# First weights in quarters, norm gains inside the constants, and five edits in the last block

## The chip, the cores and the metric

The kernel is one program on one core of a Trainium2 chip. A core has a matmul engine (TensorE, PE), a vector engine (VectorE, DVE), an activation engine (ScalarE, ACT), a general engine (GpSimd, POOL) and a queue engine that here only issues DMAs (SyncE, SP). They run beside one another and meet through semaphores. The metric is the device time of one execution in microseconds; lower is better. A run is given as the median of its executions.

## The reference, cut to what matters

256 tokens of width 1024 go through two layers and a last block. All is float32.

```python
for l in range(2):
    proj = rms_norm(x, attn_norm[l]) @ w_in[l]             # 1024 -> 2472
    ...                                                    # mLSTM, latent attention, spatial gating
    x = x + y @ w_out[l]
    x = x + hier_moe(rms_norm(x, ffn_norm[l]), ...)        # 32 experts, two for each token
# the last block
proj = rms_norm_2(x, norm_w) @ w_in_2                      # 1024 -> 6144
qa, ka, va, za, qb, kb, vb, zb, gl_a, gl_b = split(proj)   # 8 times 512, twice 1024
qa, ka = rms_norm_2(heads(qa), q_norm_w), rms_norm_2(heads(ka), k_norm_w)
oa = softmax_attention(qa, ka, va, rel_bias)               # 8 heads, bias by distance, from a table of 32 buckets
ob = stick_breaking_attention(qb, kb, vb)
ya, yb = (oa * silu(za)) @ w_up_moba, (ob * silu(zb)) @ w_up_sb
y = sigmoid(gl_a + b0) * ya + sigmoid(gl_b + b1) * yb
x = x + y @ w_out
```

## The kernel before, in words

The program keeps x on chip, as two tiles of 128 tokens (t = 0, 1). Each engine runs one long list of instructions in program order. Weights come from memory in units of up to 2 MB (a "unit" is 1024 rows by up to 512 columns) into a ring of six slots; SP issues their DMAs in a fixed order and waits before each for the slot to be given back by PE (`freed`), while PE waits for `landed`. Matmul results go to eight banks; an order written out by hand (`MIXER_BANKS`, `second_banks`) says who uses which bank when, PE waits for the bank's last reader (`open_bank`), and `copied(engine, plan, names)` makes an engine wait until the named results have been read out of their banks. A float32 product of 128x128 by 128xN is two passes of PE.

**The start.** SP's first DMAs are, in order: the first 129 columns of the constants (identity and one column of -0.5), x tile 0, the layers' norm gains (L579), the last block's gains (L580), rows 0 to 511 of unit 2 of the first projection (L583), x tile 1, rows 512 to 1023 of unit 2, then unit 3 (L649) and sixteen small loads of the mixer (L608). Constants and gains share the semaphore `loaded_first`; PE, ACT, DVE and POOL wait for 48 of it, three DMAs. PE fills the time with nine products of zeros (`keep_warm`), turns x tile 0 (L1008), ACT scales the result by the gains into `xfT` (L1706), and PE begins `b1t0`, the first result of unit 2, with its first four of eight row blocks k when `loaded_half` is there. It then turns x tile 1, does the other four blocks after `landed[2]`, and goes on with tile 1. Before the mixer's small products (L1129) it waits for all sixteen small loads; POOL waits for the same loads at L778.

**The last block: bias.** After the projections qa, ka, qb and kb, PE turns the bias table (result `rel`), DVE copies it out, PE multiplies it by a bucket matrix to get a row of 384 biases for each of 8 heads (result `f`, L1565), and DVE copies that out (L2617) and raises `f_ready`. Only then does PE multiply va and vb, two tiles each (L1523). SP, which stands at `expand_bias` between the loads of zb and ga0, waits for `f_ready` and writes the rows, each 128 times, into a scratch tensor in memory (`skew`, L701, 1536 KB), waits for that write, and reads it back with a pitch one element short, so that each partition gets its own shift (`s_bias`, L705, 1024 KB). The next four unit loads (ga0, ga1, gb0, gb1, L683) stand behind it on SP. On DVE the normalisation of q and k (L2623, L2627) follows the copy of `f`; then DVE waits for `s_bias` (`bias_moved`) and for the merge gate's bias before the first head.

**The last block: heads.** PE turns q and k (L1574), waits until ACT has copied out all of vb1, qT0, qT1, kT0, kT1 among others, and runs the steps h = 0 to 8. Step h is: `lead` chunks, `first_stage(h)` (logits of both attentions), `front` chunks, `second_stage(h - 1)` (sums of the log rows, which wait for `s_log_ready`, and the turned softmax, which waits for `s_norm_ready`), further chunks, and at every second step `third_stage` (products with v). Chunks are pieces of independent work: one eighth of a tile of za, zb, ga or gb, and `step_tiles` says how many stand where. A lead has one chunk. DVE adds the bias to head h's logits (L2666), gets the maximum, ACT takes the exponential (L1981), DVE scales the rows by the sum (L2656, L2657).

**The end.** The products with w_up (L1657) are gated on DVE to y, turned by PE (`turn_y`, L1645), copied out by ACT, and multiplied with w_out in four results out0 to out3 of 128x512 (L1672). y tile 1 is turned after out1. DVE adds each result to x (L2739). SP stores x tile 0 (512 KB) after out1 and x tile 1 (512 KB) after out3 (L724).

Of the kernel before, what the change touches and what calls it, by code (L numbers as in the profile page):

```python
# [21 lines left out]
P = 128  # L22
SEQ = 256
NT = SEQ // P
D = 1024
# [12 lines left out]
FIRST_CONSTS = P + 1  # L38
# [27 lines left out]
CONST_WIDTHS = [("ident", P), ("neg_half", 1), ("upto", P), ("before", P), ("fromon", P), ("ones", P), ("iota", P),  # L66
# [19 lines left out]
def step_tiles(h):  # L86

    def pieces(first, last):
        out = []
        while first < last:  # L90
            stop = min(last, (first // KD + 1) * KD)
            out.append((TILES[first // KD], first % KD, stop - first // KD * KD))
            first = stop
        return out

    front = h * KD + max(h - 1, 0) * BACK_CHUNKS
    back = front + KD - (TAIL_CHUNKS if h == S_HEADS else 0)
# [10 lines left out]
def second_banks():  # L108
    uses = [("rs", 6), ("rel", 4), ("f", 5)]
    uses += [(n, b) for names in (("qa0", "qa1", "ka0", "ka1"), ("qbA", "qbB", "kbA", "kbB"),  # L110
                                  ("va0", "va1", "vb0", "vb1")) for b, n in enumerate(names)]
    uses += [("qT0", 4), ("qT1", 5), ("kT0", 6), ("kT1", 7)]
    tile = 0

    def opened(pieces):
        nonlocal tile
        for name, k0, _ in pieces:
            if k0 == 0:
                uses.append((name, tile % 4))
                tile += 1  # L120

    for h in range(S_HEADS + 1):
        if h < S_HEADS:
            uses += [(f"z{h}", 4 + h % 2), (f"sc{h}", 6 + h % 2)]
        lead, front, behind, tail = step_tiles(h)
        opened(lead + front)
        if h:
            uses += [(f"r{h - 1}", 4 + (h - 1) % 2), (f"pT{h - 1}", 6 + (h - 1) % 2)]
        opened(behind)
        if h and h % 2 == 0:  # L130
            uses += [(f"ob{h // 2 - 1}", 5), (f"oa{h // 2 - 1}", 7)]
        opened(tail)
    uses += [(f"y{a}{t}{n}", 2 * (n % 2) + (a == "b")) for t in range(2) for n in range(2) for a in "ab"]
    uses += [(f"yT{u}", 4 + u) for u in range(4)] + [(f"out{b}", b) for b in range(4)]
    return uses


def constant_table():
# [18 lines left out]
        "row_limit": np.where(p == 0, SEQ - 1.0, NO_TOKEN),  # L157
        "piece": np.concatenate([(p + P * c) // M_DIM == h for h, c in PIECES], axis=1),
# [41 lines left out]
def program(nc, io, out, mixer=True, second=True):  # L200
    with ExitStack() as ctx:
# [11 lines left out]
        at = 0  # L213
        for name, w in CONST_WIDTHS:
            const[name] = consts[:, at:at + w]
            at += w
# [19 lines left out]
        gain_cols = sb("gain_cols", [P, DEPTH + 1, KD])  # L236
# [179 lines left out]
        loaded_half = sem("loaded_half")  # L416
# [31 lines left out]
        loaded_merge_bias = sem("loaded_merge_bias")  # L448
# [139 lines left out]

# [140 lines left out]
        def _(pool):  # L729
# [33 lines left out]
            for l in range(DEPTH):  # L763
                m = PER * l
                if mixer:
                    if l == 0:
                        pool.wait_ge(loaded_first, 48)
# [102 lines left out]
        def _(pe):  # L870
# [124 lines left out]
            pe.wait_ge(loaded_first, 48)  # L995
# [26 lines left out]
            def mix(l):  # L1022
# [16 lines left out]
                def token_unit(u, name, t, k0=0, k1=KD, release=None):  # L1039
# [5 lines left out]
                    if l == 0 and name == "b1t0" and k0 == 0:  # L1045
                        pe.wait_ge(loaded_half, 16)
                    elif k0 == 0 or name == "b1t0":
                        lands(u, 1)
# [64 lines left out]
                token_unit(2, "b1t0", 0, 0, 4)  # L1113
# [355 lines left out]
            def last_block():  # L1469
# [107 lines left out]
                copied(pe, plan, "qbA", "qbB", "kbA", "kbB", "va0", "va1", "vb0", "vb1", "qT0", "qT1", "kT0", "kT1")  # L1577
# [104 lines left out]
        def _(act):  # L1682
# [14 lines left out]
            def norm_turn(m):  # L1697

                if m == 0:
                    act.wait_ge(loaded_first, 48)  # L1700
                    act.activation(stats[:, 15:16], ident[:, 0:1], ACT.Copy)
# [304 lines left out]
        def _(dve):  # L2006
# [505 lines left out]
            dve.wait_ge(loaded_first, 48)  # L2512
# [70 lines left out]
            def last_block():  # L2583
# [64 lines left out]
                dve.wait_ge(loaded_merge_bias, 16)  # L2648
# [85 lines left out]
                for t in range(NT):  # L2734
                    for n in range(2):
                        name = f"out{2 * t + n}"
                        src = full(dve, plan, name)
                        xs = x[:, t, n * HALF:(n + 1) * HALF]
                        dve.tensor_tensor(xs, xs, src[:, :], ALU.add).then_inc(left(plan, name), 1)  # L2739
                        copied(dve, plan, name)  # L2740
                        if (t, n) == (0, 1):
# [32 lines left out]
```

## Time and profile before

| | |
|---|---|
| median of 3 runs | 1051.71 us (1049.93 to 1052.14) |
| profiled execution | 1053.72 us |
| its span, first to last instruction | 1051.5 us |
| PE busy / DVE / ACT / POOL | 98% / 38% / 27% / 9% |
| chain that ended last | PE 88%, SP's queue 7%, DMA 2%, ACT 1%, DVE 1% |
| mean granted PE clock | 0.998 |
| read from memory | 286.99 MB, 277 GB/s over the span |

Busy shares are of the span. The chain that ended last is followed back from the last instruction, at each step to what released it. A granted clock of 1.00 is 2.4 GHz, of 0.50 1.2 GHz. In a timeline each row gives the start and the length in microseconds, the engine, the line, the operation, what it writes and reads, how many instructions are merged, and in brackets how long the engine had been idle before and what ended that.

### The profile page before, as it was taken

What the parts mean: (1) busy time and instruction counts of PE and PEld (TensorE: products, weight loads), DVE (VectorE), ACT (ScalarE), POOL (GpSimd) and SP (SyncE); (2) the same over time, 40 slices, a digit from 0 to 9 for tenths busy, and PEclk for the clock granted to TensorE, in tenths of its full rate; (3) what the DMA queues carried; (4) which work ended last, traced back from release to release, by engine and by line L of the source; (5) the groups of instructions that cost most, each with busy time, mean ns of one, the idle gap of its engine ahead of it and who ended that gap; (6) DMA issues with size and microseconds to landing.
All of it is one profiled execution on the core that took longest, in us unless ns stands there. A gap on an engine that the chain in (4) does not pass through costs nothing.

```text
span 1051.5 us, 12900 instructions
## 1 busy us (share of the span) xinstructions
PE 1031.5 (98%) x4599; PEld 535.9 (51%) x4599; DVE 397.2 (38%) x970; ACT 279.3 (27%) x540; POOL 97.9 (9%) x144
## 2 busy tenths in 40 slices
PE   8999999999999999999999999999999999999998
PEld 4787654333333434777654333333334756855443
DVE  2362343443344441452343444344431221445221
ACT  4355331111111113354341111111112004565200
POOL 1320221000000002210220000000000200000000
PEclk9999999999999999999999999999999999999999
DMA  8646258999999997245258999999979626842000
GB/s 294 223 147 253 80 200 307 411 411 413 412 411 411 414 368 241 74 176 225 81 201 324 412 411 413 413 411 412 414 300 368 253 29 148 324 161 80 0 1 40
DMA packets 95325, 280.44 MB, mean 267 GB/s; under 512 B 15957, under 2 KB 29699, under 8 KB 86960
## 3 DMA queue, kind: packets, MB, share of 16 engines
q1 hardware_dynamic: 90208, 273.27, 68.5%
q0 software_dynamic: 5072, 6.56, 1.8%
q8 instruction: 29, 0.48, 0.2%
q14 instruction: 16, 0.13, 0.0%
HBM read 286.99 MB, written 4.72 MB: 277 GB/s over the span
## 4 chain that ended last, share of the span: by engine, by line
PE 88%; SPq 7%; DMA 2%; ACT 1%; issue 1%; DVE 1%; DVEq 0%; ACTq 0%
PE bank L935 17%; PE bank L1523 11%; PE bank L964 9%; PE bank L1051 9%; PE bank L886 6%; SPq L598 5%; PE bank L1254 5%; PE bank L1066 4%; PE bank L875 3%; PE bank L1501 3%; PE bank L1672 3%; PE bank L1541 3%; PE bank L1657 3%; DMA ring<-in_w 2%; SPq L604 1%
## 5 line engine op out<-in xcount | busy, mean ns | idle before, releaser
L935 PE MATMUL bank<-ring,arena 128*64 128x512 f32 x1024 | 228.5, 596 | 1.5 <-DMA ring<-in_w 1.5
L935 PEld LDWEIGHTS bank<-ring,arena 128*64 128x64 f32 x1024 | 71.1, 137 | 132.8 <-issue 124.1
L964 PE MATMUL bank<-ring,arena 128*64 128x512 f32 x512 | 116.9, 598 | 0.0
L1523 PE MATMUL bank<-ring,xfT 128*128 128x512 f32 x256 | 113.4, 596 | 0.0
L1051 PE MATMUL bank<-ring,xfT 128*128 128x384 f32 (+2 forms) x256 | 96.1, 526 | 2.5 <-DMA ring<-in_w_in 2.5
L886 PE MATMUL bank<-arena 128*128 128x512 bf16 x384 | 93.3, 379 | 0.0
L1694 ACT ACTIVATE arena<-bank 128x512 bf16<-128x512 f32 (+1 forms) x64 | 38.2, 597 | 190.4 <-PE bank L964 190.4
L2025 DVE TENSOR_TENSOR arena<-bank,arena 128x512 f32<-128x512 f32 x60 | 41.5, 691 | 119.4 <-ACT arena L1694 119.4
L1523 PEld LDWEIGHTS bank<-ring,xfT 128*128 128x128 f32 x256 | 47.4, 190 | 55.5 <-issue 55.0
L964 PEld LDWEIGHTS bank<-ring,arena 128*64 128x64 f32 x512 | 33.9, 136 | 68.4 <-issue 68.4
L1051 PEld LDWEIGHTS bank<-ring,xfT 128*128 128x128 f32 x256 | 47.7, 192 | 40.0 <-issue 26.6
L1687 ACT ACTIVATE arena<-bank,arena 128x256 f32<-128x256 f32 x32 | 15.2, 475 | 198.6 <-PE bank L935 198.5
L839 POOL DMA_INDIRECT arena<-x_store,arena x30 | 30.7, 1024 | 370.8 <-PE bank L875 355.3
L2046 DVE SCALAR_TENSOR_TENSOR arena<-arena,bank 128x256 f32<-128x256 f32 x32 | 15.4, 480 | 113.2 <-ACT arena L1687 113.2
L1254 PE MATMUL bank<-ring,xfT 128*128 128x512 f32 x128 | 57.4, 596 | 0.0
L875 PEld LDWEIGHTS bank<-consts,arena 128*128 128x128 f32 x240 | 31.3, 195 | 48.7 <-issue 48.7
L886 PEld LDWEIGHTS bank<-arena 128*128 128x128 bf16 x384 | 37.8, 99 | 32.5 <-issue 1.6
L1066 PE MATMUL bank<-xfT,ring 128*128 128x256 f32 x192 | 43.0, 380 | 0.0
L875 PE MATMUL bank<-consts,arena 128*128 128x128 f32 x240 | 42.7, 300 | 0.0
L2037 DVE TENSOR_TENSOR arena<-bank,row_gain 128x512 f32<-128x512 f32 x60 | 41.2, 687 | 3.5
L1066 PEld LDWEIGHTS bank<-xfT,ring 128*128 128x128 f32 x192 | 36.2, 190 | 5.3
L2031 DVE TENSOR_TENSOR arena<-arena 128x512 bf16<-128x512 f32 x60 | 38.5, 682 | 0.0
(383 smaller groups left out, 1161.6 us busy)
## 6 DMA issues: line engine op xcount, KB each, us to landing
ring<-in_w SPq DMA_DIRECT2D x256, 512.0 KB
ring<-in_w SPq DMA_DIRECT2D x64, 1024.0 KB, 12.7
ring<-in_w_in SPq DMA_DIRECT2D x14, 2048.0 KB, 19.8
ring<-in_w_in SPq DMA_DIRECT2D x8, 1536.0 KB, 13.9
ring<-in_w_out SPq DMA_DIRECT2D x6, 2048.0 KB
x_store<-x POOLq DMA_DIRECT2D x4, 512.0 KB, 6.1
ring<-in_w_up_moba SPq DMA_DIRECT2D x1, 2048.0 KB
ring<-in_w_up_sb SPq DMA_DIRECT2D x1, 2048.0 KB
```

The costliest lines, as they stand in the source:

```text
L598: sp.dma_start(up_view(s)[:, i, w].rearrange("p k f -> p (k f)"), src)\
L875: ins = pe.transpose(dst[:, i * P:(i + 1) * P], x_rows[:, buf, :].rearrange("p (i k) -> p k i", k=KD)[:, k, :], ident)
L886: ins = pe.matmul(bank[2 * t + n][:, :], onehotT[:, par, t * P:(t + 1) * P], y_parts[:, par, i, n, :], start=False, stop=False, skip_group ...
L935: ins = pe.matmul(bank[5][CELL * e:CELL * (e + 1), :], xg[:, par, 4 * h + k, at:at + CELL], view[:, e, :, k, :], start=(h == 0 and k == 0) ...
L964: ins = pe.matmul(bank[5 + n][CELL * e:CELL * (e + 1), :], turned[:, par, c, CELL * e:CELL * (e + 1)], down_view(s)[:, e, c, n * HALF:(n + ...
L1051: ins = pe.matmul(dst[:, 0:w], xfT[:, k, t * P:(t + 1) * P], unit_view(u, w)[:, k, :], start=(k == 0), stop=(k == KD - 1))
L1066: ins = pe.matmul(dst[:, at:at + SEQ], unit_view(u, M_WIDTH)[:, k, c * P:(c + 1) * P], xfT[:, k, :], start=(k == 0), stop=(k == KD - 1))
L1254: ins = pe.matmul(bank[plan[name][0]][:, :], xfT[:, k, t * P:(t + 1) * P], unit_view(n, HALF)[:, k, :], start=(first and k == ks[0]), stop ...
L1523: ins = pe.matmul(dst[:, :], xfT[:, k, t * P:(t + 1) * P], w[:, k, :], start=(k == 0), stop=(k == KD - 1))
L2025: dve.tensor_tensor(y_rest[:, n, :], bank[5 + n][:, :], y_parts[:, par, 0, n, :], ALU.subtract)\
L2031: dve.tensor_tensor(y_parts[:, par, 2, n, :], y_rest[:, n, :], y_parts[:, par, 1, n, :], ALU.subtract).then_inc(S["low_ready"], 1)
L2037: dve.tensor_tensor(xg[:, par, 4 * half:4 * half + 4, :], src[:, :].rearrange("p (k s) -> p k s", k=4), row_gain_in[:, 4 * half:4 * half + ...
```

## The change

Seven edits:

1. The three rows of norm gains (24 columns) are laid into the constants on the host, behind the column of -0.5; the first DMA brings 153 columns instead of 129, and the two gain DMAs are gone. All waits for `loaded_first` are for 16 instead of 48.
2. Unit 2's first half is loaded in two quarters (blocks k 0, 1 and 2, 3), x tile 1 after them, then the second half. `b1t0` waits for each quarter.
3. The second quarter's semaphore also serves the merge gate's bias, whose waiter on DVE now wants 32.
4. `rel` is turned after va's tile 0, `f` is multiplied after the first four blocks of va's tile 1.
5. The first step's lead has two chunks instead of one, and the wait for vb1, qT0, qT1, kT0 and kT1 stands behind it.
6. `turn_y(1)` stands between out0 and out1.
7. The last result is cut in two of 256 columns (out3, out4), and x tile 1 is stored in three parts: columns 0 to 511, 512 to 767, 768 to 1023, each after its own result.

```diff
-FIRST_CONSTS = P + 1
+FIRST_CONSTS = P + 1 + 3 * 8
...
-    lead = front + (1 if h < S_HEADS else 0)
+    lead = front + (2 if h == 0 else 1 if h < S_HEADS else 0)
...
+OUTPUTS = [[("out0", 0, 0, HALF), ("out1", 1, 0, HALF)],
+           [("out2", 0, 0, HALF), ("out3", 1, 0, HALF // 2), ("out4", 1, HALF // 2, HALF)]]
...
-        loaded_merge_bias = sem("loaded_merge_bias")
+        loaded_second_quarter = sem("loaded_second_quarter_and_merge_bias")
+        loaded_merge_bias = loaded_second_quarter
...
             sp.dma_start(x[:, 0, :], io["x"][0, 0:P, :]).then_inc(loaded_x[0], 16)
-            sp.dma_start(gain_cols[:, 0:DEPTH, :], io["attn_norm"]).then_inc(loaded_first, 16)
-            sp.dma_start(gain_cols[:, DEPTH, :], io["norm_w_2"]).then_inc(loaded_first, 16)
-            for half in range(2):
-                c0, c1 = UNIT_COLS[2]
-                sp.dma_start(unit_view(2, c1 - c0)[:, 4 * half:4 * half + 4, :],
-                             io["w_in"][0, half * HALF:(half + 1) * HALF, c0:c1].rearrange("(k p) n -> p k n", p=P))\
-                  .then_inc(loaded_half if half == 0 else landed[2], 16)
-                if half == 0:
+            c0, c1 = UNIT_COLS[2]
+            for k0, k1, signal in ((0, 2, loaded_quarter), (2, 4, loaded_second_quarter), (4, 8, landed[2])):
+                if k0 == 4:
                     sp.dma_start(x[:, 1, :], io["x"][0, P:2 * P, :]).then_inc(loaded_x[1], 16)
+                sp.dma_start(unit_view(2, c1 - c0)[:, k0:k1, :],
+                             io["w_in"][0, k0 * P:k1 * P, c0:c1].rearrange("(k p) n -> p k n", p=P)).then_inc(signal, 16)
...
-            for t in range(NT):
-
-                sp.wait_ge(x_tile_ready if t == 0 else x_ready, last)
-                sp.dma_start(out[0, t * P:(t + 1) * P, :], x[:, t, :]).then_inc(stored, 16)
-            sp.wait_ge(stored, 16 * NT)
+            parts = [(0, 0, D, x_tile_ready, last)]
+            if second:
+                parts += [(1, 0, HALF, x_tile_ready, last + 1), (1, HALF, HALF + HALF // 2, x_tile_ready, last + 2),
+                          (1, HALF + HALF // 2, D, x_ready, last)]
+            else:
+                parts += [(1, 0, D, x_ready, last)]
+            for t, c0, c1, signal, n in parts:
+                sp.wait_ge(signal, n)
+                sp.dma_start(out[0, t * P:(t + 1) * P, c0:c1], x[:, t, c0:c1]).then_inc(stored, 16)
+            sp.wait_ge(stored, 16 * len(parts))
...
-                token_unit(2, "b1t0", 0, 0, 4)
+                token_unit(2, "b1t0", 0, 0, 2)
+                token_unit(2, "b1t0", 0, 2, 4)
...
-                pe.wait_ge(loaded_second, 4 * 16)
-                pe.wait_ge(rel_ready, 1)
-                dst = open_bank("rel")
-                done(pe.transpose(dst[0:33, 0:S_HEADS], s_rel[0:S_HEADS, :], ident[0:S_HEADS, 0:S_HEADS]), "rel")
-                copied(pe, plan, "rel")
-                dst = open_bank("f")
-                done(pe.matmul(dst[0:S_HEADS, 0:384], s_relT[0:33, :], buckets[0:33, :], start=True, stop=True), "f")
-                for u in ("va", "vb"):
-                    for t in range(NT):
-                        token_tile(u, t)
...                                                # the same instructions in bias_rows() and bias_table()
+                token_tile("va", 0)
+                bias_rows()
+                token_tile("va", 1, k1=4)
+                bias_table()
+                token_tile("va", 1, k0=4)
+                for t in range(NT):
+                    token_tile("vb", t)
...
-                copied(pe, plan, "qbA", "qbB", "kbA", "kbB", "va0", "va1", "vb0", "vb1", "qT0", "qT1", "kT0", "kT1")
+                copied(pe, plan, "qbA", "qbB", "kbA", "kbB", "va0", "va1", "vb0")
...
                     chunks(lead)
+                    if h == 0:
+                        copied(pe, plan, "vb1", "qT0", "qT1", "kT0", "kT1")
...
                 for t in range(NT):
-                    if t:
-                        turn_y(t)
                     copied(pe, plan, f"yT{2 * t}", f"yT{2 * t + 1}")
-                    for n in range(2):
-                        dst = open_bank(f"out{2 * t + n}")
+                    for name, n, c0, c1 in OUTPUTS[t]:
+                        if name == "out1":
+                            turn_y(1)
+                        dst = open_bank(name)
                         for k in range(KD):
-                            ins = pe.matmul(dst[:, :], xfT[:, k, t * P:(t + 1) * P], outs[n][:, k, :],
+                            ins = pe.matmul(dst[:, 0:c1 - c0], xfT[:, k, t * P:(t + 1) * P], outs[n][:, k, c0:c1],
                                             start=(k == 0), stop=(k == KD - 1))
-                        done(ins, f"out{2 * t + n}")
+                        done(ins, name)
...
-                dve.wait_ge(loaded_merge_bias, 16)
+                dve.wait_ge(loaded_merge_bias, 32)
```

## Rows read from the trace of the kernel before

**Rows 1.** The page, busy time by engine: us, share, instructions.
```profile
PE 1031.5 (98%) x4599; PEld 535.9 (51%) x4599; DVE 397.2 (38%) x970; ACT 279.3 (27%) x540; POOL 97.9 (9%) x144
```
**Rows 2.** The chain that ended last, in order of time: start, length, what.
```profile
2.58 6.51 DMA ring<-in_w_in
...
13.17 8.54 PE bank L1051 x24
```
**Rows 3.** Timeline of SP's queue at the start.
```profile
1.63 0.42 SPq L579 DMA_DIRECT2D gain_cols<-in_attn_norm  x1
...
2.58 0.43 SPq L583 DMA_DIRECT2D ring<-in_w_in  x1
...
3.60 0.44 SPq L583 DMA_DIRECT2D ring<-in_w_in  x1
```
**Rows 4.** Windows: stretch, PE, PEld, DVE, ACT, POOL busy, PEclk, DMA share, GB/s.
```profile
4.00:4.50 0.50, 0.50 (x3) 0.20 (x2) 0.00 (x0) 0.00 (x0) 0.00 (x0) 1.00 0.84 96
```
**Rows 5.** The chain in the last block, up to head 0's second stage.
```profile
849.61 0.85 issue
...
850.88 0.81 PE bank L1565 x2
851.69 27.68 PE bank L1523 x64
...
879.39 2.65 ACT arena L1948 x5
...
898.54 0.43 PE bank L1600 x2
```
**Rows 6.** Timeline of SP's queue and DVE in the last block.
```profile
852.36 0.31 SPq L701 DMA_DIRECT2D skew<-arena  x1
...
884.27 0.36 SPq L705 DMA_DIRECT2D arena<-skew  x1
...
889.60 0.29 DVE L2666 SCALAR_TENSOR_TENSOR spare<-bank,arena 128x128 f32<-128x128 f32 x1 [31.79 <-DMA arena<-skew]
...
893.61 0.35 DVE L2657 TENSOR_SCALAR spare<-spare,arena 128x256 f32<-128x256 f32 x1
```
**Rows 7.** Timeline of PE, DVE and SP's queue at the end.
```profile
986.45 0.42 DVE L2709 TENSOR_TENSOR arena<-bank,arena 128x256 f32<-128x256 f32 x1 [2.96 <-PE bank L1620]
...
1033.56 13.97 PE L1672 MATMUL bank<-ring,xfT 128*128 128x512 f32 x32 [0.78 <-ACT xfT L1948]
...
1047.64 0.69 DVE L2739 TENSOR_TENSOR x<-x,bank 128x512 f32<-128x512 f32 x1 [6.25 <-PE bank L1672]
1048.42 0.36 SPq L724 DMA_DIRECT2D out<-x  x1
```
**Rows 8.** DMA issues at the end: count, KB each, median us to landing.
```profile
out<-x SPq DMA_DIRECT2D x2, 512.0 KB, 2.6
```
**Rows 9.** Timeline of ACT, PE and POOL at the start.
```profile
5.64 2.18 ACT L1706 ACTIVATE xfT<-bank,gain_cols 128x128 f32<-128x128 f32 x8 [0.51 <-PE bank L1008]
...
9.22 3.08 PE L1051 MATMUL bank<-ring,xfT 128*128 128x424 f32 x8 [2.53 <-DMA ring<-in_w_in]
...
10.68 0.78 POOL L742 DMA_DIRECT2D consts<-in_consts  x1 [10.25 <-DMA x<-in_x]
...
27.77 1.72 POOL L778 TENSOR_TENSOR arena<-cos_sin,arena 128x32 f32<-128x32 f32 x8 [13.64 <-DMA arena<-in_a_w_ukv]
...
28.96 0.53 PE L1129 MATMUL bank<-consts,arena 5*128 5x5 f32 x6
```
**Rows 10.** Windows in the middle of the skew write.
```profile
865.00:870.00 5.00, 5.00 (x13) 2.28 (x12) 0.00 (x0) 0.69 (x1) 0.00 (x0) 1.00 0.44 51
```
**Rows 11.** Timeline of PE where layer 1 begins.
```profile
399.10 2.64 PE L1008 MATMUL bank<-consts,x 128*128 128x128 f32 x16 [2.60 <-issue]
```
**Rows 12.** Windows of PE alone: stretch, busy, PEclk, DMA share, GB/s.
```profile
400.00:425.00 25.00, 25.00 (x81) 0.93 0.91 305
```
**Rows 13.** Windows during the last store.
```profile
1050.00:1050.50 0.50, 0.00 (x0) 0.00 (x0) 0.00 (x0) 0.00 (x0) 0.00 (x0) 1.00 1.00 410
```

More of the change, by code:

```diff
@@ L64 @@
 HALF = 512
-CONST_WIDTHS = [("ident", P), ("neg_half", 1), ("upto", P), ("before", P), ("fromon", P), ("ones", P), ("iota", P),
+CONST_WIDTHS = [("ident", P), ("neg_half", 1), ("gains", 3 * 8), ("upto", P), ("before", P), ("fromon", P), ("ones", P), ("iota", P),
                 ("causal", 2 * P), ("inv_freq", 16), ("rev", NE), ("cell64", NE),
@@ L133, in second_banks @@
     uses += [(f"y{a}{t}{n}", 2 * (n % 2) + (a == "b")) for t in range(2) for n in range(2) for a in "ab"]
-    uses += [(f"yT{u}", 4 + u) for u in range(4)] + [(f"out{b}", b) for b in range(4)]
+    uses += [(f"yT{u}", 4 + u) for u in range(4)] + [(f"out{b}", b) for b in range(5)]
     return uses
@@ L157, in constant_table @@
         "row_limit": np.where(p == 0, SEQ - 1.0, NO_TOKEN),
+        "gains": full * np.zeros((1, 3 * 8)),
         "piece": np.concatenate([(p + P * c) // M_DIM == h for h, c in PIECES], axis=1),
@@ L213, in program @@
         at = 0
+        gain_cols = consts[:, P + 1:FIRST_CONSTS].rearrange("p (m k) -> p m k", m=DEPTH + 1)
         for name, w in CONST_WIDTHS:
@@ L235, in program @@
         spare = sb("spare", [P, D])
-        gain_cols = sb("gain_cols", [P, DEPTH + 1, KD])
         rstd_row = spare[:, 6 * P:6 * P + SEQ]
@@ L415, in program @@
         loaded_first = sem("loaded_first")
-        loaded_half = sem("loaded_half")
+        loaded_quarter = sem("loaded_quarter")
         loaded_positions = sem("loaded_positions")
@@ L766, in _ @@
                     if l == 0:
-                        pool.wait_ge(loaded_first, 48)
+                        pool.wait_ge(loaded_first, 16)
                     norm(l)
@@ L994, in _ @@
             keep_warm(9)
-            pe.wait_ge(loaded_first, 48)
+            pe.wait_ge(loaded_first, 16)
             def turn(m, tiles=range(NT)):
@@ L1045, in token_unit @@
                     if l == 0 and name == "b1t0" and k0 == 0:
-                        pe.wait_ge(loaded_half, 16)
-                    elif k0 == 0 or name == "b1t0":
+                        pe.wait_ge(loaded_quarter, 16)
+                    elif l == 0 and name == "b1t0" and k0 == 2:
+                        pe.wait_ge(loaded_second_quarter, 16)
+                    elif k0 in (0, 4):
                         lands(u, 1)
@@ L1557, in last_block, with bias_rows, bias_table @@
                 pair_unit("kb")
-                pe.wait_ge(loaded_second, 4 * 16)
-                pe.wait_ge(rel_ready, 1)
-                dst = open_bank("rel")
-                done(pe.transpose(dst[0:33, 0:S_HEADS], s_rel[0:S_HEADS, :], ident[0:S_HEADS, 0:S_HEADS]), "rel")
-                copied(pe, plan, "rel")
-                dst = open_bank("f")
-                done(pe.matmul(dst[0:S_HEADS, 0:384], s_relT[0:33, :], buckets[0:33, :], start=True, stop=True), "f")
-                for u in ("va", "vb"):
-                    for t in range(NT):
-                        token_tile(u, t)
+                def bias_rows():
+                    pe.wait_ge(loaded_second, 4 * 16)
+                    pe.wait_ge(rel_ready, 1)
+                    dst = open_bank("rel")
+                    done(pe.transpose(dst[0:33, 0:S_HEADS], s_rel[0:S_HEADS, :], ident[0:S_HEADS, 0:S_HEADS]), "rel")
+                def bias_table():
+                    copied(pe, plan, "rel")
+                    dst = open_bank("f")
+                    done(pe.matmul(dst[0:S_HEADS, 0:384], s_relT[0:33, :], buckets[0:33, :], start=True, stop=True), "f")
+                token_tile("va", 0)
[5 more added lines that the diff above has]
+                    token_tile("vb", t)
                 pe.wait_ge(s_qk_ready, 1)
@@ L1699, in norm_turn @@
                 if m == 0:
-                    act.wait_ge(loaded_first, 48)
+                    act.wait_ge(loaded_first, 16)
                     act.activation(stats[:, 15:16], ident[:, 0:1], ACT.Copy)
@@ L2511, in _ @@
             dve.nop().then_inc(main["low_ready"], 2)
-            dve.wait_ge(loaded_first, 48)
+            dve.wait_ge(loaded_first, 16)
             for t in range(NT):
@@ L2734, in last_block @@
                 for t in range(NT):
-                    for n in range(2):
-                        name = f"out{2 * t + n}"
+                    for name, n, c0, c1 in OUTPUTS[t]:
                         src = full(dve, plan, name)
-                        xs = x[:, t, n * HALF:(n + 1) * HALF]
-                        dve.tensor_tensor(xs, xs, src[:, :], ALU.add).then_inc(left(plan, name), 1)
+                        xs = x[:, t, n * HALF + c0:n * HALF + c1]
+                        dve.tensor_tensor(xs, xs, src[:, 0:c1 - c0], ALU.add).then_inc(left(plan, name), 1)
                         copied(dve, plan, name)
-                        if (t, n) == (0, 1):
+                        if name in ("out1", "out2", "out3"):
                             dve.nop().then_inc(x_tile_ready, 1)
@@ L2764 @@
     arrays["consts"], arrays["late_consts"] = constant_table()
-    arrays["attn_norm"] = np.ascontiguousarray(arrays["attn_norm"].reshape(DEPTH, KD, P).transpose(2, 0, 1))
-    arrays["norm_w_2"] = np.ascontiguousarray(arrays["norm_w_2"].reshape(KD, P).transpose(1, 0))
+    gains = np.concatenate([arrays.pop("attn_norm").reshape(-1, P), arrays.pop("norm_w_2").reshape(-1, P)])
+    arrays["consts"][:, P + 1:FIRST_CONSTS] = gains.transpose(1, 0)
     io = {name: nc.dram_tensor(f"in_{name}", a.shape, mybir.dt.from_np(a.dtype), kind="ExternalInput").ap()
```

## The prediction

> **What bounds the kernel now.** I read the page first: TensorE (PE) is busy for 98% of the span [rows 1], so almost any stall of PE is paid in full and work beside PE is free until it makes PE wait. The change touches three places, and I read each as a chain of waits or a timeline.
>
> *The start.* PE's first real matmuls begin at 9.22, released by the first half of the unit, issued at 2.58 and 6.51 us under way [rows 2]. Ahead of it on SP's queue stand four DMAs; each takes a slot of about 0.47 us [rows 3]. Two of them are the gains, 12 KB in all, and the stream has a hole at 4.0 to 4.5, 96 GB/s, between x tile 0 and the weights [rows 4].
>
> *The last block.* From 849.61 to 851.69 PE works almost nothing: transpose, DVE's copy, table product [rows 5]. At 879.39 it stands behind five ACT copies, 2.65 us. A second path runs beside: the table (`f`) goes to DVE, DVE frees SP, SP issues the skew write at 852.36, and only at 884.27 the read back. DVE, idle for 31.79 us, starts head 0 at 889.60, when the read has landed [rows 6].
>
> *The end.* PE waits 0.78 us for ACT's copies before tile 1's output products; then come an add of 0.69 us, the issue at 1048.42, and 2.6 us to the landing of 512 KB [rows 7, 8].
>
> Times are of the profiled execution: 1051.5 us of span, 2.2 us around it, 1053.72 in all, 2.0 above the median 1051.71 of the three runs. I take differences and add them to the median.
>
> **The start, worked.** The first quarter is issued at 1.63, 0.95 us earlier than the half was; the second at 2.10, x tile 1 at 2.58, the last half at about 3.1 instead of 3.60 [rows 3]. The hole closes, so weights land between 0.5 (issue alone) and 0.95 us (stream shifted whole) earlier, and a quarter needs half of the bytes. PE also needs the turned x: ACT's eight copies start at 5.64 and take 2.18, the first four are out at 6.7 [rows 9]. So PE starts at about 6.9. Eight passes at 0.36 (24 in 8.54 [rows 2]) last to 9.8, the turn of tile 1 to 10.7; x tile 1, in at about 10.3 before (POOL, waiting for it, issues at 10.68 [rows 9]), is there. Next comes the last half. Before, PE found it there at 13.17. Its 0.87 MB at some 390 GB/s behind x tile 1 put its landing at 12.5; 0.5 to 0.95 earlier is 11.55 to 12.0. PE waits there, a new wait of about a microsecond, and the gain is 13.17 - 11.7 = **-1.5**. Bounds: -0.5 (it landed just at 13.17 and moves by its issue alone) and -2.4 (no wait: 13.17 - 10.75). The next place is the mixer's small loads: POOL gets them at 27.77, PE needs them at 28.96 [rows 9]; PE comes at 27.5, they at 27.3 or before, so nothing is lost. Later units wait for PE's frees, so the shift passes through. The 96 bytes more per partition in the constants and the waits for 16 instead of 48 cost nothing: PE, ACT and DVE all waited for x or for each other anyway. The merge bias wait for 32 instead of 16 counts a quarter that landed 800 us before.
>
> **The bias products.** Of the 2.08 us from 849.61 to 851.69, PE keeps the table product (two passes, 0.64 of array time at 0.43 x 384/512 each) and a small transpose (0.15); the stalls go: **-1.3**. But `f` is now made after va's tile 0 and half of tile 1: 27.68/4 + 27.68/8 + 0.2 = 10.6 us after 849.61, at 860.2 instead of 850.88 [rows 5]: 9.3 us later. Behind it on DVE wait only the q/k normalisations: they ended 31.79 before 889.60, at 857.8, now 867.1, and PE wants them at 878: free. Behind it on SP wait the skew write, the read, and the loads of ga0 to gb1, which PE needs only two heads, some 20 us, later. The write takes 31.6 us with the DMAs otherwise empty (51 GB/s, share 0.44 [rows 10]), so no neighbour slows it and nothing shortens it when it is later. DVE's start moves to 898.9, its normalised head 0, ready at 893.61 + 0.35 [rows 6], to 903.25.
>
> A rule of the Trainium skill speaks otherwise. "DMA: Bandwidth & Descriptors", section "Why a DMA increments its semaphore by 16 and not by 1", has a DMA spread over the largest number of engines, up to 16, that divides its slowest dimension: 8 here. That agrees with the share of 0.44. By the same page of the Trainium skill, section "Specifications", an engine moves about 27 GiB/s, which would make the 1.57 MB take an estimated 6.8 us, and then the delay would be hidden and the sum that of the second rival below. The row's 51 GB/s decides.
>
> **Copies' wait and the lead of two chunks.** PE's transposes now end at 879.8, the second lead chunk (0.87 each: four passes of 256 columns, half of 27.68/64 apiece [rows 5]) at 881.5, after ACT's last copy at 880.8. Head 0's products start 1.9 us earlier than before, and one chunk less stands between them and the second stage: PE would reach it at 895.8, 2.75 before 898.54; 1.3 of that are the bias stalls, **-1.45** the copies. There PE meets DVE. It stalls, first for DVE's log rows (until about 901.9), does their small products, waits for the normalised head until 903.25, and after three transposes (0.33) resumes its chunks at 903.6; before it resumed at 899.6 (the row at 898.54 and 1.2 us of stage). So the block turns from -2.75 into **+4.05**, with a PE gap of 6 us. About 0.4 more follows at head 2: its banks come free only after head 1's turn on ACT and DVE, about 4.3 us like head 0's (889.60 to 893.96), so near 907.5, where PE comes at 907.2. Bounds of the block: -2.75 (data in time) and +5.5 (write and read 1 us longer).
>
> **The clock.** After the gap of 2.60 us before 399.10 the granted clock of the stretch 400 to 425 is 0.93, so part of it went at 1.2 instead of 2.4 GHz: 25 x 0.07 = 1.75 us lost [rows 11, 12]. The gap of 2.53 us before 9.22 brought no fall: the passes after it take 0.36 for 424 columns [rows 2, 9]. No gap of 6 us is in this trace; by the nearest row I take 1.5, with bounds of 0 and 3.5 (twice that row). It overlaps the 0.4 of head 2, so block and clock are **+5.6**. The Trainium skill, "TensorE: Matmul & The Clock Gate", Part 1, says that idleness sends the array back to 1.2 GHz and work brings it up again; by that rule the fall is nearly certain, and the first rival out.
>
> **The end.** Turning y tile 1 between out0 and out1 hides ACT's copies under out1: -0.8 [rows 7]; its rows are ready on DVE long before. The last add is of 256 columns: 0.42 for 0.69, -0.27 [rows 7]. The last store is 128 KB: 384 KB less at 410 GB/s is -0.95 [rows 8, 13]; between -0.5 (a floor of 2.1 us to landing) and -0.95 I take -0.85. Two products of 256 columns instead of one of 512 are the same array time. Earlier stores are issued 3.4 us before and are out of the way. Together **-1.9**, bounds -1.2 and -2.1.
>
> **Sum.** -1.5 + 5.6 - 1.9 = +2.2: 1051.7 + 2.2 = **1053.9**.
>
> **Rivals.**
> *The clock stays up.* For it: the unpunished gap at 9.22. Against: twice as long a gap here. +4.45 in the block: +1.1, 1052.8.
> *The bias data come in time: faster.* One mechanism: the skew write takes less time when it starts later, or its landing is not what DVE waited for. It decides from a write and read shorter by 7.4 us (PE would come at 895.8, DVE's result at 903.25). Then -1.5 - 2.75 - 1.9 = -6.15: 1045.6. For it: half-used DMA engines. Against: an even 51 GB/s in an empty stretch and an idle of 31.79 that ends with that landing.
> *The start gives little.* The last half lands as before but for its issue (-0.5), and the small loads hold PE at 27.3: +3.2, 1054.9. For it: both transfers move with bytes, not with PE. Against: the hole in the stream.
>
> **How the numbers follow.** 0.2% is 2.1 us, about what this measurement can tell from none. Forecast 0.52, alone from 1052.3 to 1056; clock stays up 0.25; bias data in time 0.10; poor start 0.08; rest 0.05. The range must take in most of the first two and their unknown terms: 1050.7 to 1056.2. Above 1053.8 lie rather more than half of the forecast, the poor start and a little of the second case, 0.44; within 0.2% the rest of these, 0.44; faster 0.12.
>
> **What would show it.** PE's first weights matmul near 6.9 and a new DMA wait before the k = 4 product near 11.7. No stall around 850 and at the ACT copies. `f`'s copy 9 us later against va0, the skew write still 31.6 us, DVE idle before head 0 for about 31.8 us, and a PE stall of 6 us before the second stage of head 0, followed by a granted clock of 0.50. At the end no wait before out2, a landing under 2 us. I am wrong if the write is shorter, if no stall stands at the second stage, or if the start moves by more than 2.4 us.

## The result and the profile after

The changed kernel takes 1055.99 us (median of 5 runs, 1055.24 to 1060.11) against 1051.53 (5 runs) for the kernel before: ratio 1.0053, 95% interval 1.0040 to 1.0065. Run again later in the same form it gave 1.0048 (1.0034 to 1.0062). So it is slower by about 5 us, with 3.6 to 6.8 as what the two intervals allow. Forecast were +2.2 and a range up to 1056.2: the direction holds, the size is more than double.

The profiled execution is the slowest of the first five, 1060.11 us; its span is 1057.8. The second profile, of the repetition, took 1058.90 (span 1056.6), and stands beside the first wherever the clock matters. PE is busy 98% of the span as before [rows 1]:

```profile
PE 1036.3 (98%) x4615; PEld 541.2 (51%) x4615; DVE 397.3 (38%) x971; ACT 279.1 (26%) x540; POOL 97.9 (9%) x144
```

*Start.* PE's timeline of the changed kernel (start, length, engine, line, operation, out<-in, count, idle before and what ended it):

```profile
7.16 3.11 PE L1061 MATMUL bank<-ring,xfT 128*128 128x424 f32 x8
10.11 1.04 PE L1016 MATMUL bank<-consts,x 128*128 128x128 f32 x8
11.50 2.73 PE L1061 MATMUL bank<-ring,xfT 128*128 128x424 f32 x7 [0.36 <-DMA ring<-in_w_in]
...
27.53 0.53 PE L1140 MATMUL bank<-consts,arena 5*128 5x5 f32 x6
```

The first weights matmul starts 2.06 us earlier than the one at 9.22 [rows 9]. A new wait for a DMA stands before k = 4, the second half of the unit, and what followed at 13.17 [rows 2] follows at 11.50. The small transposes stand at 27.53 instead of 28.96 [rows 9]. These are differences of one profile from one; several profiles of either start make them smaller, as worked out below.

*The last block.* The chain of the changed kernel between va and head 0's second stage (start, length, what):

```profile
849.33 6.87 PE bank L1534 x16
856.19 0.12 PE bank L1574
856.32 3.63 PE bank L1534 x8
859.95 0.75 PE bank L1579 x2
...
861.35 33.63 DMA skew<-arena
894.98 0.02 issue
895.00 5.92 DMA arena<-skew
...
903.63 0.30 DVE arena L2704
...
904.07 1.19 PE bank L1619 x2
...
906.76 4.98 PE bank L1512 x16
```

The stalls of [rows 5] around the bias products are gone. The chain now runs over DMAs: `f` at 859.95, the skew write at 861.35 instead of 852.36, the read at 895.00 instead of 884.27 [rows 6], head 0's log rows (L2704) ready at 903.94. What PE waited for in this stretch (engine and line, releaser: total, times, longest):

```profile
PE bank L1619 <- DVE arena L2704: 8.4, 1, 8.4
```

PE came at 904.07 - 8.4 = 895.7, where the forecast had 895.8. DVE was later than forecast. The windows show the clock (stretch, PE busy, PEclk, DMA share, GB/s):

```profile
900.00:904.00 4.00, 0.00 (x0) 0.50 1.05 388
904.00:910.00 6.00, 5.93 (x18) 0.52 1.05 387
```

The granted clock is already at the 1.2 GHz level while PE stands, and the work behind the wait runs at it: the stage's first two products take 1.19 us, and 16 chunk products 4.98.

*The end*, timeline of the changed kernel, and its DMA issues (KB each, us to landing):

```profile
1034.29 20.81 PE L1693 MATMUL bank<-ring,xfT 128*128 128x512 f32 x64
...
1055.13 0.42 DVE L2759 TENSOR_TENSOR x<-x,bank 128x256 f32<-128x256 f32 x1 [3.03 <-PE bank L1693]
```
```profile
out<-x SPq DMA_DIRECT2D x2, 128.0 KB, 1.8
```

PE no longer waits before tile 1's products, which was 0.78 us [rows 7], the last add is 0.42 instead of 0.69, and the last store lands in 1.8 us instead of 2.6 [rows 8].

**One yardstick for all traces.** I cut each profiled execution at two places that every kernel here has: where the last block's norm begins on PE (16 turns of x, at 791.85 before), and where the first 12 products with the unit ga0 begin behind head 2's turn (918.35 before). Between them lies "the block", behind the second "the end". In us, as differences from the kernel before (126.50 and 133.15):

```
kernel                        block    end     skew write
changed, first profile        +8.83   -2.24   33.6
changed, second profile       +7.82   -2.2    33.6
bias products late, alone     +6.20   -0.1    31.9
bias products back            -1.52   -2.2    33.6
start edits alone              0.00   -0.1    34.45
copies' wait and lead alone   -1.52    0.0    31.9
end edits alone                0.00   -2.2    31.9
```

The block and the end repeat to 0.1 us where nothing is late, so the profiles split what the times, which scatter by 3 us, can't.

### The profile page after: what moved, and what is told of

Its sections match the earlier page's. It is cut to its first block, busy times and chain, and to the rows that moved or that the text cites. A ratio compares the mean times of both kernels' runs of the same rounds, so it can differ in the third digit from the quotient of the medians.

```text
span 1057.8 us, 12934 instructions
## 1 busy us (share of the span) xinstructions
PE 1036.3 (98%) x4615; PEld 541.2 (51%) x4615; DVE 397.3 (38%) x971; ACT 279.1 (26%) x540; POOL 97.9 (9%) x144
## 4 chain that ended last, share of the span: by engine, by line
PE 77%; SPq 12%; DMA 8%; issue 2%; ACT 1%; DVE 0%; DVEq 0%; ACTq 0%
PE bank L943 14%; SPq L601 9%; PE bank L1534 9%; PE bank L1061 8%; PE bank L972 7%; PE bank L894 5%; PE bank L1265 5%; PE bank L1076 4%; DMA ring<-in_w 3%; DMA skew<-arena 3%; SPq L607 3%; PE bank L1552 3%; PE bank L1693 3%; PE bank L1678 3%; PE bank L883 2%
```

## The experiments

Ratios are to runs of the kernel before, taken beside each experiment on the same chip; 0.001 is 1.05 us. Code is cut at "...".

**Bias products back** in front of va, all else changed.

```diff
-token_tile("va", 0)
 bias_rows()
-token_tile("va", 1, k1=4)
 bias_table()
-token_tile("va", 1, k0=4)
-for t in range(NT):
-    token_tile("vb", t)
+for u in ("va", "vb"):
+    for t in range(NT):
+        token_tile(u, t)
```

> The changed kernel with the bias products back ahead of va, all other edits kept. Theory (the late table costs the time): the skew write starts near 851 again, head 0 on DVE near 889, no PE wait at the second stage of head 0, clock 1.00 there. In the changed kernel's trace that block cost 8.8 us against before; here it should give 1.4 to 2.7 back instead of costing, so 1047 to 1048 if the start's 1.4 us are lost in the expert phases, 1045.6 if they stand. Rival (the lead of two chunks and the moved copies' wait, or the end, make it slower): it stays above 1052.

Measured: 1047.38 us, ratio 0.9968 (0.9955 to 0.9981). With the table in its old place the other edits make the kernel faster, by 2.0 to 4.7 us. Its profile has no wait at the second stage.

**Bias products late, alone**: the kernel before with edit 4 only.

> The kernel before with the bias products moved behind va's tile 0 and half of tile 1, and nothing else. Theory: PE is 1.3 ahead, the table 9.3 later; PE waits before the second stage of head 0 by about 7 us, the granted clock falls, and the whole costs +6 to +9: 1057.5 to 1060.5. If the clock costs nothing, +5. Rival (the wait needs the other edits): within 2 us of before.

Measured: 1057.38 us, ratio 1.0064 (1.0050 to 1.0077), a loss of 5.3 to 8.1 us. PE waits 5.1 us at the second stage, less than the 7 expected. Together with the run that took this edit back, it shows that this edit is the cause of the slowdown. Its block, +6.20, is 1.6 to 2.6 below the changed kernel's; 1.7 of that is its skew write of 31.9 us.

**Start edits alone** (1 to 3).

> The kernel before with the start's edits alone (gains in the constants, quarters, the shared semaphore). Theory (the expert phases end on the stream of weights, which does not come earlier by as much): PE is 1.4 ahead at the mixer's small products (27.6 instead of 29.0), still at 130 us, and 0 to 0.4 ahead when the first expert phase ends near 393; total -0.5 to 0. Rival (the gain passes through): total -1.4, 1050.1.

Measured: 1050.04 us, ratio 0.9997 (0.9989 to 1.0006): -1.2 to +0.6 us. The forecast's -1.5 lies outside. So does the rival's -1.4. And its trace had something that I hadn't looked for: the skew write took 34.45 us, not 31.9.

**Zeros in the wait**: the changed kernel with 30 products of zeros ahead of head 0's second stage.

```diff
+if h == 1:
+    dst = open_bank("zb0")
+    for _ in range(30):
+        pe.matmul(dst[:, :], zeros[:, 0:P], zeros, start=True, stop=True)
 if h:
     second_stage(h - 1)
```

> The changed kernel with 30 bf16 products of zeros (128x128 by 128x512, 6.5 us at 0.216) put before the second stage of head 0, into a bank that is not in use. Theory (part of the cost is the clock after an idle PE): PE still resumes only when DVE's data come, but the granted clock stays 1.00, r0's products take 0.8 us instead of 1.6 and the chunks behind 3.5 instead of 5.0: 2 to 3 us less than the changed kernel, 1053 to 1054. Rival (the clock costs nothing, only the wait): the same as the changed kernel, 1056.

Measured: 1055.92 us, ratio 1.0049 (1.0033 to 1.0064). PE's timeline and the windows of this kernel:

```profile
895.55 6.42 PE L1656 MATMUL bank<-consts 128*128 128x512 bf16 x29
903.53 0.67 PE L1619 MATMUL bank<-arena,consts 128*128 128x256 f32 x2 [1.56 <-DVE arena L2708]
```
```profile
900.00:904.00 4.00, 2.44 (x12) 1.00 1.05 387
904.00:910.00 6.00, 5.65 (x33) 1.00 1.05 387
```

The clock stays at 2.4 GHz, and the block is +6.35 instead of +7.8 and +8.8, a difference of 1.5 and 2.5 us. Some 0.3 us of either is not the clock: against the block's start, DVE began head 0 11.30 us later than in the kernel before, and 11.55 and 11.63 later in the two profiles of the changed kernel. That leaves 1.2 and 2.2 us for the fall. The expected 1053 to 1054 did not come: the times of six runs don't show a gain, and the interval is about that of the changed kernel. So the clock's share is known from profiles only. Kept warm, the kernel is still at least 3.5 us slower than before: most of the loss is the late data.

**Once more, unaltered.**

> The changed kernel once more, unaltered, for a second profile beside the first and for the experiments of this call. The first profile was 4 us above the median of its kernel. Expected: 1056 median, skew write 33.6 us, PE's wait at the second stage 8.4 us. If what the clock took (3.0 us in the first profile) is fixed by the length of the wait, it is 3.0 here; if it depends on where the wait falls, it is anything from 0.5 to 3.

Measured: 1055.94 us. PE's wait and the windows of the second profile:

```profile
PE bank L1619 <- DVE arena L2704: 8.3, 1, 8.3
```
```profile
900.00:904.00 4.00, 0.21 (x1) 0.59 1.05 388
904.00:910.00 6.00, 6.00 (x24) 0.70 1.05 386
```

The same wait, but the clock is back sooner: the chain has the 16 chunk products at 4.05 us instead of 4.98, and the block is 1.0 shorter. The length of the wait doesn't fix what the clock costs. The expected median and wait came; the 3.0 us for the clock were too much.

**End edits alone** (6 and 7), and **copies' wait and lead alone** (5).

> The kernel before with only the end changed: y's tile 1 turned between out0 and out1, the last output in two halves of 256 columns, tile 1 stored in three parts. The two traces show the end 2.2 us shorter with all edits in. If it stands by itself: 2.0 to 2.3 us below the kernel before. Rival: part of the 2.2 belonged to the clock of the last stretch, then 1 us or less. Second use: its skew write. If the write of 33.6 us comes with the start's edits, it is 31.9 us here; if it scatters from run to run, it may be anything between 31.9 and 34.5.

> The kernel before with only the wait for ACT's copies moved behind a lead of two chunks. PE comes 1.3 to 1.45 us earlier to head 0, but in the kernel before it resumes at 899.6 only 4.7 us after DVE could have head 0 ready (893.96), so nothing meets it: theory 1.3 us faster than the kernel before. Rival: the time comes back at a later head, then no change. Its skew write is 31.9 us if the start's edits lengthen it, anything between 31.9 and 34.5 if it scatters.

Measured: 1049.69 us, ratio 0.9990 (0.9977 to 1.0003), and 1050.12 us, 0.9995 (0.9982 to 1.0008). Both intervals reach from about no change to beyond the expected gain. By the profiles, the end is 2.2 shorter in the first and the block 1.52 in the second. The skew writes were 31.9 in both: it does not scatter, it is longer where the start's edits are in.

**The arena moved** by 96 bytes: the kernel before with `gain_cols` allocated ahead of the arena, no instruction changed.

```diff
+gain_cols = sb("gain_cols", [P, DEPTH + 1, KD])
 late = ctx.enter_context(nc.sbuf_tensor("arena", [P, ARENA], F32))
...
 spare = sb("spare", [P, D])
-gain_cols = sb("gain_cols", [P, DEPTH + 1, KD])
```

> The kernel before with the gain columns' tile placed ahead of the arena instead of behind it, so that the arena and all in it lie 96 bytes further, as in the changed kernel; the instructions are the same. Theory (the longer skew write, 33.6 to 34.4 us in the four kernels with the start's edits against 31.9 in the two without, comes from where the arena lies): the write takes 33.6 us here. Rival (it comes from the DRAM side or from the order of the loads): 31.9 us. In either case the write is covered here and the time is within 1 us of the kernel before; if the moved arena also slows the expert phases' stream, up to 1 us slower.

Measured: 1050.86 us, ratio 0.9999 (0.9989 to 1.0009). SP's queue:

```profile
851.76 0.31 SPq L701 DMA_DIRECT2D skew<-arena  x1
885.38 0.36 SPq L705 DMA_DIRECT2D arena<-skew  x1
```

885.38 - 851.76 = 33.62 us, against 31.91 in [rows 6]. The place of the arena, and so of the source rows, alone lengthens the write by 1.7 us. In the kernel before this is hidden; in the changed one it is paid. The gains inside the constants (edit 1) widen the constants' tile by 96 bytes, and the arena follows it.

**The arena first**, aligned to 512 bytes, all else as changed.

```diff
+late = ctx.enter_context(nc.sbuf_tensor("arena", [P, ARENA], F32))
+spare = sb("spare", [P, D])
 consts = sb("consts", [P, sum(w for _, w in CONST_WIDTHS)])
...
-late = ctx.enter_context(nc.sbuf_tensor("arena", [P, ARENA], F32))
...
-spare = sb("spare", [P, D])
```

> The changed kernel with arena and spare placed ahead of the constants' tile, so that the arena begins at a multiple of 512 bytes and the source rows of the skew write with it; before, they began 360 bytes behind such a multiple, in the changed kernel 456. Same instructions. Theory (the write's duration goes by how its source rows lie): neither 33.6 nor a scatter but another fixed duration; if fewer 64-byte or 512-byte pieces per row help, below 31.9 us, perhaps 29 to 31. The time then falls by the same amount below the changed kernel, 2 to 4 us, since DVE waits for that landing: 1052 to 1054. Rival (only a shift of the DRAM side): 33.6 us and 1056.

Measured: 1055.43 us, ratio 1.0045 (1.0031 to 1.0059). SP's queue, and what PE waited for:

```profile
858.38 0.32 SPq L704 DMA_DIRECT2D skew<-arena  x1
890.34 0.36 SPq L708 DMA_DIRECT2D arena<-skew  x1
```
```profile
PE bank L1619 <- DVE arena L2704: 6.7, 1, 6.7
```

The write is back at 31.96 us and PE's wait 1.6 shorter than in the changed kernel. The block is +7.36, only 0.5 below the changed kernel's second profile: DVE began head 0 9.94 us later than in the kernel before, and by the yardstick of the kernel with zeros the clock took 2.4 us here. The expected 29 to 31 did not come: an aligned row is as slow as one that begins 360 bytes behind a multiple of 512, and only the one at 456 is slower. A time gain of 1 us or less can't be told here. The Trainium skill, "DMA: Bandwidth & Descriptors", section "How a descriptor splits into AXI transactions", counts 32-byte beats from the 256-byte boundary below the start. For rows of 1536 bytes that makes 52, 55 and 48 beats for the three places. 55 to 52 is 1.058, and 33.6 to 31.9 is 1.054: agreed. 48 should have given an estimated 29.5 and gave 31.96: not agreed. What holds the aligned write at 31.96 is open.

**The same write from 128 partitions**: the table copied to 128 rows, 8 reads of each instead of 128 reads of 8. The product `f` has 128 columns of weights for it, and the scratch tensor is laid out head first, so that the eight copies of a row lie one behind the other in memory instead of 12 KB apart.

```diff
-skew = nc.dram_tensor("skew", [P, S_HEADS, 384], F32, kind="Internal").ap()
+skew = nc.dram_tensor("skew", [S_HEADS, P, 384], F32, kind="Internal").ap()
...
-sp.dma_start(skew.rearrange("p h j -> h p j"),
-             s_f[0:S_HEADS, :].unsqueeze(1).broadcast_to([S_HEADS, P, 384])).then_inc(bias_moved, 16)
+sp.dma_start(skew.rearrange("h (c q) j -> (h c) q j", c=16),
+             s_f[0:128, :].unsqueeze(1).broadcast_to([128, P // 16, 384])).then_inc(bias_moved, 16)
...
```

> The changed kernel with the bias table copied to 128 partitions (the product has 128 columns of weights instead of 8), the skew tensor head first, and the write reading 128 source rows eight times each instead of 8 rows 128 times each. The same 1.57 MB. Theory (the write is slow because only 8 engines work on it, at some 6.4 GB/s each): share of the DMAs rises from 0.44 to about 0.9 and the write takes 16 us; theory b (the single source partition limits, not the engine): the write takes 4 to 6 us. Both free PE at the second stage: no wait there, no fall of the clock, and the block is 2.75 us shorter than in the kernel before, so the time is 8 to 9 us below the changed kernel, some 4.5 to 5.5 below the kernel before. Rival (the write is limited by its target, 1024 rows of 1.5 KB in DRAM): still 31 to 34 us, and the time is that of the changed kernel.

Measured: 1045.65 us, ratio 0.9953 (0.9935 to 0.9970): faster than both kernels. SP's queue, and the windows during the write:

```profile
860.27 0.64 SPq L704 DMA_DIRECT2D skew<-arena  x1
866.31 0.38 SPq L708 DMA_DIRECT2D arena<-skew  x1
```
```profile
861.00:865.00 4.00, 4.00 (x11) 1.00 0.88 319
```

6.0 us for the same 1.57 MB, at 319 GB/s instead of 51 [rows 10]. Twice as many DMA engines would have made it 16 by the share alone (0.88 for 0.44), and 1024 rows of 1.5 KB are written as before; so neither the count of engines nor that of the rows bound it. Two things are left, the eight partitions read and the order in which the rows lie in memory, and no run parts them. For the source speaks that its place alone changed the write by 1.7 us. The Trainium skill has the rule, "SBUF — State Buffer", section "Door 1: The DMA port swizzle": DMA bandwidth goes by how many of 16 ports the partitions reach, and partitions 0 to 7 reach two. By its 435 GB/s over 16 ports that is an estimated 54 GB/s; the trace agrees, with 51 in [rows 10]. PE has no wait at the second stage, and the block is -2.45.

**Bias products earlier**: in the second half of qb, the slow 8-row write kept.

```diff
-pair_unit("qb")
...
-token_tile("va", 0)
-bias_rows()
-token_tile("va", 1, k1=4)
-bias_table()
...
+pair_unit("qb", {(1, 0): bias_rows, (1, 1): bias_table})
...
```

DVE's two copies of the bias results move with them, between its work on qb's two halves.

> The changed kernel with the bias rows' transpose and the table product moved the other way: into the second half of qb's products, some 28 us earlier than in the changed kernel and 20 us earlier than in the kernel before. The 8-row write is untouched (33.6 us). Theory (only the landing time of the skew data against head 0 counts): write issued near 833, read back near 873, no wait at the second stage, no stall around 850, the block 2.5 to 2.8 us shorter than in the kernel before, time 1045.5 to 1047. Rival (the work itself costs PE or DVE time wherever it stands, or it delays the first-block turns on DVE): 1048 or more.

Measured: 1044.63 us, ratio 0.9942 (0.9928 to 0.9956), also faster than both. SP's queue:

```profile
833.26 0.32 SPq L704 DMA_DIRECT2D skew<-arena  x1
866.88 0.37 SPq L708 DMA_DIRECT2D arena<-skew  x1
```

The write still takes 33.6 us, but it starts 28 us earlier, PE waits nowhere, and the block is -2.5. With a faster write or an earlier one the loss is gone: what counts is its landing against head 0.

**PE late by four**: the kernel before with 40 products of 256 bf16 columns ahead of the first layer's small transposes.

> The kernel before with 40 extra products of 256 bf16 columns (0.11 us each, 4.3 us in all) in the first layer, ahead of the small transposes that stand at 28.96 in its profile. The extra products are overwritten. Theory a (a shift of PE at the start passes through to the end, as the prediction had it): 4.3 us slower, 1054.8 to 1055.3, and every milestone (first expert issue at 162.3, second router at 399.1, third at 791.9) moves by 4.3. Theory b (the expert phases, paced by the weight stream, take it up): the first milestone moves by 4.3, the second by less than 2, and the time by 0 to 2.

Measured: 1055.59 us, ratio 1.0042 (1.0028 to 1.0055), +2.9 to +5.8. Two rows of its PE timeline and one of SP's queue between them:

```profile
28.53 4.53 PE L1131 MATMUL bank<-consts 128*128 128x256 bf16 x40
```
```profile
166.35 1.87 SPq L598 DMA_DIRECT2D ring<-in_w  x4
```
```profile
404.09 2.33 PE L1008 MATMUL bank<-consts,x 128*128 128x128 f32 x15 [2.58 <-issue]
```

The first expert unit is issued 4.0 later than before and layer 1 begins 5.0 later: a delay of PE at the start passes through, and the expert phases take none of it up. That an advance passes through as well is not shown by it.

## Why the prediction was right in kind and wrong in size

**The start, -1.5: mis-sized.** The local steps came as written: PE near 6.9 (7.16), a new DMA wait near 11.7 (11.50), the small transposes 1.43 earlier. But both numbers are of one profile each. Over the five profiles with the old start the small transposes stand at 28.20 to 28.96, mean 28.52; the forecast had taken the latest. Over the eight with the new start they stand at 26.94 to 28.66, mean 27.60. The typical gain is 0.9, and the first expert unit's issue has 0.8 of it (162.05 to 161.24, means of the same five and eight). The new wait of "about a microsecond" stands in four of the eight, with 0.17 to 0.91 us. The step "the shift passes through" is shown for a delay only, by the run that is late by four. Of the gain, the means have 0.4 left where layer 1 begins (399.20 to 398.81) and 0.3 at the last block's norm (791.24 to 790.92), where single profiles of the new start lie between 788.60 and 792.38. So 1.5 was too much already at the start, and how much of the 0.9 arrives at the end is open; 0.3 and 0.9 both fit the -1.2 to +0.6 of the start edits alone.

**The bias products, -1.3 and 9.3 us later: right.** The stalls are gone, `f` comes 9.1 later (859.95 for 850.88).

**"The skew write still 31.6 us", DVE at 898.9: this step failed.** DVE started head 0 at 900.94 (900.66 in the second profile, whose block began 0.49 earlier than that of the kernel before), and PE waited 8.4 us where 6 was forecast. The write took 1.7 us more and the read 0.5 to 0.6. Why the read did is open: in the twelve profiles in which DVE's head 0 waited for it, it took 5.26 to 6.70 us from its issue to DVE's start. The longer write has its root in a sentence of the start's part: the 96 bytes more per partition "cost nothing". As instructions they did; but they moved the arena, and with it the source of a DMA that had had 5.8 us to spare. In the kernel before, DVE's log rows of head 0 were ready at 892.58, and PE wanted them at 898.54 [rows 5]:

```profile
892.29 0.29 DVE L2683 TENSOR_TENSOR arena<-arena 128x128 f32<-128x128 f32 x1
```

The 9.3 us of edit 4, and the 2.75 by which PE comes earlier, used that up, so every further microsecond of the DMAs was paid. The bound of +5.5, "write and read 1 us longer", was too close for that: they were 2.3 longer.

**Copies' wait and lead, -1.45: right alone, worth nothing here.** PE came at 895.7 as forecast, and the block was 1.52 shorter in the kernel with this edit alone. In the changed kernel it only lengthens the wait. That was in the sum, which took PE's time as the smaller of the two.

**The clock, 1.5: right within its scatter.** It fell after the wait, as forecast. In the second profile PE resumes its chunks behind the second stage at 906.27, which against the start of the block is 7.16 later than before. 4.05 of that is the forecast's stall and 2.26 the landing (1.72 write, 0.54 read); the remaining 0.85 is the second stage at 1.2 GHz. After it 0.66 more goes in the chunks, to the block's 7.82. By the forecast's own terms, then, the clock took 1.5 there and 2.5 in the first profile; the kernel with zeros makes it 1.2 and 2.2. That a term of 1.5, taken from a gap of 2.6 us, fits a wait of 8.3 so well is luck in part, since the first profile of the same kernel has 1 us more. The 0.4 at head 2 did not show by itself.

**The end, -1.9: a little more, -2.2,** in every kernel with edits 6 and 7. The parts are those of the forecast; the landing gave 0.8, PE's wait 0.8, the add 0.27, and the rest is not split.

**The sum.** With 0.3 to 0.9 for the start and the second profile's block, -0.9 + 7.8 - 2.2 = +4.7 to -0.3 + 7.8 - 2.2 = +5.3, against a measured 4.2 to 6.8 and 3.6 to 6.5. From the forecast's +2.2 it is 2.2 for the block, nearly all of it the landing, 0.6 to 1.2 for the start and -0.3 for the end; nothing that these times could tell is left over for another cause.

**The rivals.** *The clock stays up*: no, 0.50 is granted. *The bias data come in time*: not here; its condition was a write and read 7.4 us shorter, its price 1045.6. The write from 128 partitions fulfils the condition (some 26 us shorter than the 31.6) and gives 1045.65. That the two times agree so closely is in part luck: against the runs of the kernel before beside it the change is -4.9 (-3.2 to -6.8), and the price was -6.15, with 1.5 for the start in it. The support that I had taken for it, half-used DMA engines, named the wrong limit: at a share of 0.44 they moved 51 GB/s in all, and at 0.88, in the kernel with 128 partitions, 319. The partitions read, or the order of the rows written, were the limit. *The start gives little*: its size was half right, but not by its mechanism: the second half landed earlier, and the small loads held no one.

## What to carry to other kernels

When work is moved later to fill a stall, follow its result through every queue and DMA to the one that waits for it: the stall filled here was 1.3 us, and the chain behind it had some 6 us to spare when 9 were taken. Before fitting the schedule around a slow DMA, look at how its source and target lie: the same bytes took 31.9 us from eight partitions and 6.0 from 128. An edit that changes a tile's width moves all tiles behind it: compare the durations of DMAs that touch them, and take a gain at the start from several profiles, since one can lie 0.4 to 1 us off the mean; then follow it on to the end, since a gain at the start need not arrive there.

## What the runs showed of the hardware that I had not expected

- A write of 1024 rows of 1.5 KB to memory takes 31.9 us from eight partitions and 6.0 us from 128 (with the rows in another order in memory).
- With the same eight partitions, it takes 33.6 us where the rows begin 456 bytes behind a multiple of 512, but 31.9 us at 360 and 32.0 at 0 (the places are worked out from the sizes of the tiles allocated ahead; no trace shows them). One kernel, the start edits alone, took 34.45 at 456; why is open.
- Waits of 8.4 and 8.3 us at the same place cost, by a clock at 1.2 GHz behind them, 2.2 and 1.2 us, and one of 6.7 us in the kernel with the arena first cost 2.4 (against the kernel with zeros). Filled with products of zeros down to 1.6 us idle, the clock stays at 1.00.
